# A two-block transformer kernel: inputs and vectors in the layout the engines read, modulation weights in one run per partition and first in the queue

## The reference, cut to what matters

```
act_lat, act_ctx = silu(c), silu(c_ctx)
sh, sc, gt = split(act @ w_ada[0] + b_ada[0], 3)       # "modulation", w_ada: 2 x 1024 x 3072
u = rms_norm(h, norm_g[0]) * (1 + sc) + sh             # for x with act_lat, for ctx with act_ctx
p = u @ mla_w_in
```

## Time and profile before

| | us |
|---|---|
| median of three runs | 1284.62 (1284.25 to 1284.8) |
| the profiled execution | 1285.15 |
| its span, first to last instruction | 1283.4 |
| TensorE busy | 1271.1 (99%) |
| VectorE, ScalarE, GpSimd busy | 818.3, 655.3, 448.8 |

### The profile page before, as it was taken

One profiled execution on the slowest core, in us unless ns is written; L12 is line 12 of the kernel. 1 busy time (PEld: TensorE's weight loads), 2 busy tenths in 40 slices (PEclk: granted clock), 3 DMA queues, 4 the chain that ended last, 5 costly groups with the idle time before them and its releaser, 6 DMA issues.

```text
span 1283.4 us, 17458 instructions
## 1 busy us (share of the span) xinstructions
PE 1271.1 (99%) x6553; PEld 1065.3 (83%) x6553; DVE 818.3 (64%) x1208; ACT 655.3 (51%) x1066; POOL 448.8 (35%) x212
## 2 busy tenths in 40 slices
PE   9999999999999999999999999999999999999998
PEld 4688888889988888888789889888888888888886
DVE  1796788764945457789658335406448678667686
ACT  5543777744523354766655534632355534545341
POOL 0243011137433394522244334344663322333210
PEclk9999999999999999999999999999999999999999
DMA  9972001076332153322223233233354233332301
GB/s 348 322 241 75 11 23 33 18 246 187 97 99 66 34 164 99 99 53 63 65 70 96 83 82 83 78 93 94 96 164 154 84 124 99 107 107 82 115 1 66
DMA packets 181401, 135.43 MB, mean 106 GB/s; under 512 B 10154, under 2 KB 154651, under 8 KB 181324
## 3 DMA queue, kind: packets, MB, share of 16 engines
q1 hardware_dynamic: 181122, 134.34, 34.5%
q10 hardware_dynamic: 202, 0.06, 0.0%
HBM read 129.66 MB, written 4.72 MB: 105 GB/s over the span
## 4 chain that ended last, share of the span: by engine, by line
PE 88%; DVE 4%; ACT 4%; DMA 2%; POOL 1%; issue 1%; ACTq 0%; DVEq 0%; SPq 0%; POOLq 0%
PE psum L2379 27%; PE psum L2381 26%; PE psum L2380 26%; PE psum L2437 2%; PE psum L2593 2%; DMA w_raw<-in_fno_w_in 1%; PE psum L2581 1%; PE psum L2582 1%; POOL w_lo L784 1%; ACT w_hi L903 1%; DVE m_probs L2031 1%; DVE m_turned_lo L2036 0%; PE psum L2530 0%; DMA w_raw<-in_mla_w_out 0%; DMA vec_rows<-in_moba_k_norm_g 0%
## 5 line engine op out<-in xcount | busy, mean ns | idle before, releaser
L784 POOL TENSOR_TENSOR w_lo<-w_raw,w_hi 128x1024 fp32r<-128x1024 f32 x148 | 383.6, 2598 | 641.0 <-ACT w_hi L903 605.7
L2379 PE MATMUL psum<-u_hi,w_hi 128*128 128x512 f32 (+1 forms) x704 | 265.2, 377 | 1.0 <-DVE u_lo L1837 0.6
L2381 PE MATMUL psum<-u_hi,w_lo 128*128 128x512 f32 (+1 forms) x704 | 260.9, 371 | 0.0
L2380 PE MATMUL psum<-u_lo,w_hi 128*128 128x512 f32 (+1 forms) x704 | 260.7, 370 | 0.0
L903 ACT ACTIVATE w_hi<-w_raw 128x1024 fp32r<-128x1024 f32 x148 | 155.0, 1053 | 72.2 <-PE psum L2381 28.1
L2379 PE MATMUL psum<-y_hi,w_hi 128*128 128x512 f32 x416 | 162.2, 390 | 0.0
L2381 PE MATMUL psum<-y_hi,w_lo 128*128 128x512 f32 x416 | 161.9, 389 | 0.0
L2380 PE MATMUL psum<-y_lo,w_hi 128*128 128x512 f32 x416 | 161.9, 389 | 0.0
L2379 PEld LDWEIGHTS psum<-u_hi,w_hi 128*128 128x128 f32 x704 | 132.8, 189 | 23.5 <-POOL w_lo L784 1.2
L2381 PEld LDWEIGHTS psum<-u_hi,w_lo 128*128 128x128 f32 x704 | 132.6, 188 | 23.2
L2380 PEld LDWEIGHTS psum<-u_lo,w_hi 128*128 128x128 f32 x704 | 132.9, 189 | 21.0 <-issue 0.2
(11 more groups left out here) (511 smaller groups left out, 2591.2 us busy)
## 6 DMA issues: line engine op xcount, KB each, us to landing
w_raw<-in_w_in SPq DMA_DIRECT2D x52, 512.0 KB, 3.8
w_raw<-in_w_up SPq DMA_DIRECT2D x32, 512.0 KB, 4.1
down_set<-in_w_down SPq DMA_DIRECT2D x32, 512.0 KB, 4.8
ada_back<-in_w_ada SPq DMA_DIRECT2D x7, 2048.0 KB, 11.2
w_raw<-in_fno_w_in SPq DMA_DIRECT2D x16, 512.0 KB, 3.9
ada_w<-in_w_ada SPq DMA_DIRECT2D x3, 2048.0 KB, 14.3
w_raw<-in_mla_w_in SPq DMA_DIRECT2D x11, 512.0 KB, 5.2
w_raw<-in_mla_w_out SPq DMA_DIRECT2D x8, 512.0 KB, 3.9
```

The source lines that it names most:

```text
L784: pool.tensor_tensor(WL[:, j, :], RAW[:, j % 2, :], f(WH[:, j, :]), ALU.subtract).then_inc(lo_done, 1)
L2379: pe.matmul(out, ah, bh, start=first, stop=False, skip_group_check=more)
L2380: pe.matmul(out, ah, bl, start=False, stop=False, skip_group_check=more)
L2381: return pe.matmul(out, al, bh, start=False, stop=last, skip_group_check=more)
```

## The change

It does these things together:

- On the host, `x` and `ctx` are given with features on rows, the vectors as one 128-partition array of columns, and `w_ada` with the 16 KB that a partition needs of a quarter in one run.
- The loads: columns, quarter 0 in halves, quarters 2 and 1, then `x` straight into `HT`, quarter 3 in halves, then the weight tiles and `ctx`. Bias table and identity go through ScalarE's queue, the 15 vector loads are gone.
- TensorE no longer turns `x`, the vectors and `ctx`, and warms up with 12 products in place of 18.
- The sums of squares now run over partitions and chunks: ScalarE squares whole chunks, VectorE adds the eight chunks to one, and TensorE adds over partitions (for `x` four products with two columns, whose root and reciprocal feed `DIAG` as before; for `ctx` one product with 256 columns, spread over all partitions at once).
- The modulation's matmuls are reordered around these sums (quarter 1 has four `QHI` products, the turn of row 1, four more, then eight `QLOW` products, and quarter 3 comes in three pieces), and tiles 0 and 1 are no longer interleaved in chunks 0 to 3.
- `ctx_e` multiplies by the spread 1/rms, and the shift is added in `UCH` and `UCL`.
- The load of the second later quarter (`gate_load(1)`) waits for the sum of `ctx` squares.

```diff
 # SyncE
-            sp.dma_start(IDENT[:], d["identity"]).then_inc(s_const, 16)
-            for n in range(2):
-                sp.dma_start(XTOK[:, 2 * n:2 * n + 2, :], ...).then_inc(s_x[n], 16)
...
+            sp.dma_start(COLS[:, 0:NROWS], d["columns"]).then_inc(s_cols, 16)
+            ada_halves(0, s_first)
+            for q in (2, 1):
+                sp.dma_start(AQ[q][:], ada_weights(q)).then_inc(s_adaq[q], 16)
             for n in range(2):
+                sp.dma_start(HT[:, 4 * n:4 * n + 4, :], ...).then_inc(s_x[n], 16)
+            ada_halves(3, s_last)
...
-            sp.wait_ge(row_ss, TT + 1)
-            sp.wait_ge(x_t, KC)
+            sp.wait_ge(in_sum, 2)
             gate_load(1)
 # ScalarE
             ada_row_copy(0, 0, 1)
+            act.wait_ge(s_adaq[1], 16)
+            second_hi(0)
+            second_hi(1)
             ada_row_copy(1, 2, 2)
...
+            second_hi(2)
+            second_hi(3)
+            x_squares(0)
+            x_squares(1)
...
             ada_row_copy(2, 1, 4)
+            x_squares(2)
+            x_squares(3)
+            act.wait_ge(spread_mm, 2)
+            act.activation(RSC[:, 0:TT], bank(0, 2 * TT)..., ACT.Sqrt, ...).then_inc(in_sq, 1)
             split_hi(A0, None, 0)
...
-            for m in range(TC // P):
-                act.wait_ge(row_ss, TT + 1 + m)
-                act.activation(JUNK[:], CTOK[:, m, :], ACT.Square, accum_out=...).then_inc(row_ss, 1)
...
+            act.wait_ge(in_sum, 1)
+            for n in range(2):
+                act.activation(CSQ[:, 4 * n:4 * n + 4, :], CTX[:, 4 * n:4 * n + 4, :], ACT.Square).then_inc(in_sq, 1)
             for c in range(4, KC):
                 lat_hi(c)
             split_hi(A0, None, 2)
-            act.wait_ge(row_ss, 9)
-            for m in range(TC // P):
-                act.activation(CTOK[:, m, :], CTOK[:, m, :], ACT.Copy, scale=...).then_inc(x_scaled, 1)
+            act.wait_ge(spread_mm, 4)
+            act.activation(CRSTD[:], bank(6, TC), ACT.Sqrt, scale=1.0 / D, bias=EPST[:]).then_inc(in_sq, 1)
             act.wait_ge(kv_raw[1], 16)
             split_hi(A0, None, 3)
 # VectorE
+            for n in range(2):
+                v.wait_ge(in_sq, 2 * n + 2)
+                a, b = slice(4 * n, 4 * n + 2), slice(4 * n + 2, 4 * n + 4)
+                link(v.tensor_tensor(XSQ[:, a, :], XSQ[:, a, :], XSQ[:, b, :], ALU.add))
+            link(v.tensor_tensor(XSQ[:, 0:2, :], XSQ[:, 0:2, :], XSQ[:, 4:6, :], ALU.add))
+            v.tensor_tensor(XSUM[:], XSQ[:, 0, :], XSQ[:, 1, :], ALU.add).then_inc(in_sum, 1)
+            v.wait_ge(in_sq, 5)
+            link(v.reciprocal(RSC[:, 0:TT], RSC[:, 0:TT]))
+            for m in range(TT):
+                v.tensor_scalar(DIAG[:, m, :], IDENT[:], RSC[:, m:m + 1], None, ALU.mult).then_inc(q_lo1, 1)
...
+            v.wait_ge(in_sq, 7)
+            link(v.tensor_tensor(CSQ[:, 0:4, :], CSQ[:, 0:4, :], CSQ[:, 4:8, :], ALU.add))
+            link(v.tensor_tensor(CSQ[:, 0:2, :], CSQ[:, 0:2, :], CSQ[:, 2:4, :], ALU.add))
+            v.tensor_tensor(CSUM[:], CSQ[:, 0, :], CSQ[:, 1, :], ALU.add).then_inc(in_sum, 1)
...
             def ctx_chunks():
+                v.wait_ge(in_sq, 8)
+                link(v.reciprocal(CRSTD[:], CRSTD[:]))
 # TensorE
-            for _ in range(18):
+            for _ in range(12):
                 pe.matmul(bank(6, P), ONES[:], ONES[:], start=True, stop=True)
...
             ada(2)
+            pe.wait_ge(s_const, 16)
+            turn_row(0, 0)
...
...
+            ada(3, 0, 4)
+            pe.wait_ge(in_sum, 1)
+            pe.wait_ge(bias_row, 3)
+            for m in range(TT):
+                mm = pe.matmul(bank(0, 2, 2 * m), XSUM[:, m * P:(m + 1) * P], ONES[:, 0:2], start=True, stop=True)
+            mm.then_inc(spread_mm, 1)
+            ada(3, 4, 6)
+            pe.wait_ge(q_lo1, 4 + TT)
             for m in range(TT):
                 mm = pe.matmul(bank(3, P, m * P), ONES[:], DIAG[:, m, :], start=True, stop=True)
             mm.then_inc(spread_mm, 1)
+            ada(3, 6, KC)
...
+            for k in range(4):
+                pe.wait_ge(u0_lo, k + 1)
+                lat_step(0, k)
+                if k == 1:
+                    pe.wait_ge(mod_done, 1)
+                    last_columns()
             pe.wait_ge(lo_done, 2)
+            for k in range(4):
+                lat_step(1, k)
+            for k in range(4, KC):
                 pe.wait_ge(u0_lo, k + 1)
...
             for j in range(2, 4):
                 pe.wait_ge(lo_done, j + 1)
                 for k in range(KC):
                     mm = lat_step(j, k)
-                    if j == 3:
-                        turn_ctx(k)
+                if j == 2:
+                    pe.wait_ge(in_sum, 2)
+                    pe.wait_ge(u0_hi, KC)
+                    pe.matmul(bank(6, TC), ONES[:], CSUM[:], start=True, stop=True).then_inc(spread_mm, 1)
```

More of the change, by code:

```diff
@@ L927, in _, with x_squares @@
             act.activation(CSPLIT[:, :, 0:2], CACT[:], ACT.Copy).then_inc(cact_done, 1)
[L928 to L939, removed]
+            act.activation(DUMMY[:, 0:1], EPST[:], ACT.Sqrt)
+            def x_squares(n):
+                act.wait_ge(s_x[n // 2], 16)
+                act.activation(XSQ[:, 2 * n:2 * n + 2, :], HT[:, 2 * n:2 * n + 2, :], ACT.Square).then_inc(in_sq, 1)
             def ada_row_copy(n, q, done):
@@ L956, in _ @@
             ada_row_copy(2, 1, 4)
+            x_squares(2)
+            x_squares(3)
+            act.wait_ge(spread_mm, 2)
+            act.activation(RSC[:, 0:TT], bank(0, 2 * TT).rearrange("p (m n) -> p m n", n=2)[:, :, 0], ACT.Sqrt, scale=1.0 / D, bias=EPST[:])\
+                .then_inc(in_sq, 1)
             split_hi(A0, None, 0)
@@ L1617, in _ @@
                 if half == 0:
[L1618 to L1619 removed]
+                    v.wait_ge(spread_mm, 3)
                 first_modulation(half)
@@ L2434, in ada @@
                 for k in range(k0, k1):
-                    if q == 0 and k == 4:
-                        pe.wait_ge(s_first, 16)
+                    if q in (0, 3) and k == 4:
+                        pe.wait_ge(s_last if q else s_first, 16)
                     mm = pe.matmul(ada_row_bank(q)[0:2, :], CACT[:, k, :], AQ[q][:, k, :], start=k == 0, stop=k == KC - 1)
@@ L2457, in _ @@
             ada(2)
-            pe.wait_ge(diag_done, TT)
+            pe.wait_ge(s_const, 16)
+            turn_row(0, 0)
+            pe.wait_ge(cact_done, 4)
+            for k in range(KC):
+                pe.wait_ge(q_hi1, k // 2 + 1)
+                pe.matmul(ada_row_bank(1)[0:4, :], CSPLIT[:, k, :], QHI[:, k, :], start=k == 0, stop=False)
+                if k == 3:
+                    turn_row(1, 2).then_inc(ada_mm, 1)
+            for k in range(KC):
+                pe.wait_ge(q_lo1, k // 2 + 1)
+                mm = pe.matmul(ada_row_bank(1)[0:2, :], CSPLIT[:, k, 0:2], QLOW[:, k, :], start=False, stop=k == KC - 1)
+            mm.then_inc(ada_mm, 1)
+            ada(3, 0, 4)
[6 more added lines that the diff above has]
+            pe.wait_ge(q_lo1, 4 + TT)
             for m in range(TT):
@@ L2461, in _ @@
             mm.then_inc(spread_mm, 1)
-            turn_row(0, 0)
-            turn_row(1, 2).then_inc(ada_mm, 1)
-            pe.wait_ge(cact_done, 4)
-            for k in range(KC):
-                pe.wait_ge(x_copied, KC + k // 2 + 1)
-                pe.matmul(ada_row_bank(1)[0:4, :], CSPLIT[:, k, :], QHI[:, k, :], start=k == 0, stop=False)
-            for k in range(KC):
-                pe.wait_ge(diag_done, TT + k // 2 + 1)
-                mm = pe.matmul(ada_row_bank(1)[0:2, :], CSPLIT[:, k, 0:2], QLOW[:, k, :], start=False, stop=k == KC - 1)
-            mm.then_inc(ada_mm, 1)
-            ada(3)
+            ada(3, 6, KC)
             def last_columns():
@@ L3149 @@
     nc = _bacc.Bacc("TRN2", target_bir_lowering=False, num_devices=1)
-    arrays, d = {}, {}
+    arrays, vectors, d = {}, {}, {}
     vec_of = {v: k for k, v in _VEC_INPUTS.items()}
@@ L3155 @@
         if name in vec_of:
-            key = vec_of[name]
-            a = a.reshape(-1, MD if key in ("q_norm", "k_norm") else P)
+            vectors[vec_of[name]] = a.reshape(-1, MD if vec_of[name] in ("q_norm", "k_norm") else P)
+            continue
+        if name in ("x", "ctx"):
+            a = _np.ascontiguousarray(a.reshape(-1, D).T)
+        elif name == "w_ada":
+            a = _np.ascontiguousarray(a.reshape(2, KC, P, 6, T).transpose(0, 3, 2, 1, 4))
         elif a.ndim == 3 and a.shape[0] == 1:
@@ L3161 @@
         d[key] = nc.dram_tensor(f"in_{name}", a.shape, _mybir.dt.from_np(a.dtype), kind="ExternalInput").ap()
+    rows = [_np.tile(vectors[name], (1, 2)) if name in ("q_norm", "k_norm") else vectors[name] for name, _ in VECS]
+    arrays["in_columns"] = _np.ascontiguousarray(_np.concatenate(rows).T)
+    d["columns"] = nc.dram_tensor("in_columns", (P, NROWS), _mybir.dt.float32, kind="ExternalInput").ap()
```

134 lines of the change are left out of this document (37 added, 97 removed).

## The result

The changed kernel took 1292.0 us as a median of five runs (1289.71 to 1293.14), against 1284.62 before (1284.14 to 1284.8): a ratio of 1.0054, interval 1.004 to 1.0067. It is slower by 7.4 us, where I forecast 1.4, and outside the range. The profiled execution took 1293.14 with a span of 1291.3.

The account below looks back on a forecast made before the run. TensorE, busy 99%, bounds the kernel: leads of 1.5 and 1.4 against a 4.1 wait put context products 1.3 later; with 0 to 0.5 for chunks and 0.3 back near 317, +1.4, 1286.0, range 1283.3 to 1289.0.

Parts of the forecast that it names:

- rival B: Wait before tile 3 also drops TensorE's clock, so tile 3 starts at half pace: 2.5 more, +3.9, 1288.5; chance 0.24.
- `ada(0)` 6.5: Entry: first modulation products start at 6.5, when quarter 0's first half lands, 6.3 earlier than before.
- Low products over at 26.5: Entry: quarter 1's last low products end at 26.5 instead of 34.98, a lead of 8.5.
- sum of `x` 32.3: Entry: ScalarE's squares and VectorE's adds for `x` are finished at 32.3, ahead of TensorE's sum.
- the lead of 1.5: End of the entry: tile 2 starts at 52.8 in place of 54.34.
- `ada(3, 0, 4)`: Entry: quarter 3's first piece waits for its weights until 28.2 and ends at 31.7.
- The wait before tile 3: Between context sum and tile 3, TensorE idles 4.1 us for root, high part and low part; bounds 3.5 to 4.5.
- VectorE's adds held by GpSimd: Adds of `ctx` squares wait until GpSimd finishes splitting tile 2 at 51.7, ending at 54.0, before TensorE asks at 58.3.
- Context chunks late by 0 to 0.5: VectorE's last context chunk is ready at 71.3, TensorE wants it at 70.8: 0 to 0.5 more.
- The 0.3 near 317: Later quarters' longer runs may land sooner and shrink TensorE's idle time near 317 by 0.3.
- C, the sums hidden after all: Rival: the entry is bound by TensorE's own list, a lead of 5.7, -3.0 in all, 1281.6; chance 0.08 with the faster cases' 0.48/0.24/0.20 rivals.
- the leads of 1.5 and 1.4: Gains before the context products: 1.5 from tile 2 starting earlier, 1.4 from no longer turning the context.

Follow-up runs that it names:

- the run with both waits filled: Changed kernel with its own orders, plus unused-output dummy products on TensorE in all entry waits and the wait for the context's root: 1286.93 us.
- 1.7 in the kernel before: Kernel before, with ScalarE's split of tile 3 made to wait until TensorE finished tile 2: 1290.04 us; with 16 dummy products in that wait, 1288.3.
- the run with only the entry filled: Changed kernel with 18 unused-output dummy products in three idle stretches of TensorE before 44 us: 1289.55 us.
- With `x` loaded first: Kernel with orders mended, `x` loaded, squared and summed before quarter 1, and dummy products at that sum and before quarter 1's products: 1282.73 us.
- the run with the split first: Changed kernel with ScalarE's high part of tile 3 moved ahead of its wait for the context sum: 1290.29 us.
- with only the wait of tile 3 filled: Changed kernel with 17 unused-output dummy products between the context's sum and the wait for tile 3: 1289.84 us.
- the mended kernel without products of ones: Changed kernel with context sum after six steps of tile 2, tile 3's split before the root, context chunks before the modulation sum, no dummy products: 1287.65 us.

## Why the prediction was wrong

**The step that failed** is the pricing of TensorE's idle times in the entry: "Chunk 0 is ready at 39.7, chunk 1 at 41.1. TensorE idles for 1.8 and 0.7", taken at their own length and at nothing for the clock; and rival B, with 0.24, priced a lost clock only for the wait of tile 3 and, in an aside, for the start of `ada(0)` (where nothing was lost: its 16 records take 7.03, as before). In the profiled execution the clock took 4.5 in the entry: 58.81 for tile 2, against 54.12 in the run with both waits filled (its context sum at 59.57 less the eight steps), less the 0.2 by which that run started sooner: 1.5 behind the idle of 2.25 and 3.0 behind that of 1.72. Behind the wait of tile 3 it took 1.3 (68.78 to 75.70 is 6.92, 64.10 to 69.72 is 5.62). Together that is 5.8 in this execution, the longest of its five; by medians it is 5.1. How it divides changes from execution to execution: the medians of the runs with one of the two filled give 2.5 for the entry and 2.2 for the wait. The trace before left the point open. The prediction read that no gap in it was near 4 us, and gave its own waits of 1.7 (26.5 to 28.2), 0.6 (31.7 to 32.3) and 1.8 no clock, though in that trace TensorE never stood for more than 0.33 between 13 and 84, so that nothing there showed such times to be free either. By the prediction's own signs (tile 2 after 54) it was wrong: tile 2 started at 58.81, and with the clock kept at 54.12.

Step by step, predicted and measured:

- `ada(0)` 6.5, measured 7.26 (6.82 to 7.39 in the other runs of this layout). The first half of quarter 0 landed 5.9 after its issue (5.5 to 6.0 in the others) in place of the 5.3 of the earlier trace rows.
- Low products over at 26.5, measured 27.56; sum of `x` 32.3, measured 33.38 (VectorE's last add starts at 32.69 and takes 0.69). All but 0.3 of it is the late start handed on. With the clock kept, first step 40.89 for 39.7 and tile 2 at 54.12 for 52.8: the lead of 1.5 was only 0.2.
- `ada(3, 0, 4)` was to wait for quarter 3 until 28.2. It started at 27.59 with no wait, so that the two waits told for this place, 1.7 and 0.6, became the one of 2.25 before the sum of `x`: as long in all, but in one piece.
- The wait before tile 3: predicted 4.1. From the context's sum to the first step of tile 3 it is 4.53, of which the sum was to take 0.44: 4.09. The chain came as told, ScalarE's root and split, then GpSimd. The timeline of ScalarE after:
```profile
64.89 0.47 ACT L963 ACTIVATE ctx_rstd<-psum,eps 128x256 f32<-128x256 f32 x1 [11.71 <-PE psum L2485]
65.26 1.05 ACT L899 ACTIVATE w_hi<-w_raw 128x1024 fp32r<-128x1024 f32 x1
```
- Pace of tile 3's steps: B's sign, 1.36 apart, measured 1.45 and 1.28 (68.78, 70.23, 71.51), and then 0.78 and 0.69. B priced 2.5 and it was 1.3 here, 1.7 in the kernel before and 2.3 in the run with only the entry filled. B had the mechanism, with a size near the largest of these; what it lacked was the entry.
- VectorE's adds held by GpSimd: told, and seen: 3.34 for an add that takes 1.23 with GpSimd at rest. The Trainium skill (SBUF — State Buffer, the section on SBUF's two separate sides) states that a VectorE operation with two inputs in SBUF and a GpSimd one that reads SBUF exclude each other for a whole instruction; the trace agrees: GpSimd's split runs from 53.25 to 55.65, the add starts at 53.38 and ends 1.07 behind the split.
- Context chunks late by 0 to 0.5: in the changed kernel 0, since TensorE came 7 later than thought. The order of VectorE's list was a true fault all the same: without any wait ahead of tile 3 and with the entry filled the kernel took 1289.5, and 1283.62 once the chunks and the sum stood earlier too.
- The 0.3 near 317: the shift falls by 0.4 between 286 and 339, as told. The wait for `u_lo` at 317.42 before, 0.59, is gone, and there is one of 0.54 for `w_lo` at 308.44.
- C, the sums hidden after all: no. TensorE stood 2.25 for the sum. With `x` loaded first they nearly are, and the first latent step still came at 40.53, 3.1 behind C's 37.4. The 1282.73 of that run is not C's 1281.6 come true: C has the wait of 4.1 in it, and in that run the wait is gone.

Summed for the context products of the profiled execution: 1.3 predicted, 1.4 of sizes (1.3 of them in the entry), 4.5 of clock there, 0.2 of its own later start, 1.3 of clock behind tile 2: 8.7, as measured. The wait of 4.1 was right; of the leads of 1.5 and 1.4 set against it, the first was 0.2. What is left of wait and leads without the clock, 2.4 by medians, is a third of the loss. The Trainium skill (TensorE: Matmul & The Clock Gate, Why this matters for your kernels) warns of idle gaps between bursts of matmuls, as the prediction cites it. The traces agree at 3.93 and 3.62, which are long enough for its warning; its words do not reach the shorter ones, and there the measurement decides: the clock fell behind idle times of 1.05 to 2.32 too.

## What to carry to other kernels

Where TensorE is the bound, an idle time on its list costs its own length, and it can cost a stretch at half the clock on top: here 1.3 to 3 us for each drop, behind idles of 1.05 to 3.9. Price both, look at the granted clock and for records longer than their like, and if a wait can't be taken away, fill it; eighteen short products were worth 4 us. When a wait is taken out of one engine's list, read the next engine's list for what is put ahead of the thing now needed, before you count the gain.

## What the runs showed of the hardware that I had not expected

- Whether an idle time costs the clock is not settled by its length: 2.25 us before the sum of `x` was followed by 0.54 in the changed kernel, 2.27 at the same place by 1.00 in the run with the split first; 1.72 before the first latent step by a drop in the changed kernel and by none with only the wait of tile 3 filled; 1.05 near 111 cost it in one execution, and a row of waits of 0.3 in another. What else decides stays open. It goes far to explain the spread of runs of one program, 1285.98 to 1291.54 for the mended kernel without products of ones, but not all of it: one run with the split first took 1290.09 at a mean clock of 0.999, while the fastest, 1289.69, had 0.996.
- The lower level sometimes starts late: behind the idle of 1.72 that ended at 42.56 the first step ran at full pace, and 0.50 came at 44.4.
- A first megabyte in rows of 8 KB landed 5.5 to 6.0 after issue in the ten profiled executions that have it, one in rows of 4 KB after 5.1 to 5.7 in four. Small loads of another queue landed 1.2 later in the one profile of the kernel before with long rows.
